# Two gathers of a mixture-of-experts pair, from both sides of an up stage to behind it and to the end of the pair

## The chip, the cores and the metric

The kernel runs on one core of a Trainium2 chip. The metric is the device time of one execution in microseconds (us); less is better. The core has a matrix engine (TensorE, PE in the profile), a vector engine (VectorE, DVE), an activation engine (ScalarE, ACT), a general one (GpSimd, POOL) and a queue that issues the weight loads (SyncE, SP). PEld is TensorE's loading of the stationary operand.

## The reference, cut to what matters

Two decoder layers run on 512 tokens of width 1024. Each has a mixer, a cross-attention to 256 memory tokens and a mixture of experts. The change touches the last alone:

```python
xs = xf[tok]
h = jax.nn.silu(lax.ragged_dot(xs, w_gate, sizes)) * lax.ragged_dot(xs, w_up, sizes)
y = lax.ragged_dot(h, w_down, sizes) * weights.reshape(-1)[order][:, None]
out = jax.ops.segment_sum(y, tok, num_segments=T)
```

There are 32 experts in a layer, and each token goes to two of them. An expert has three float32 matrices of 2 MB (`w_gate`, `w_up` of 1024x512, `w_down` of 512x1024).

## The kernel before, in words

**Pairs and stages.** Experts are taken two at a time: 16 pairs `q` in a layer, 64 token slots for each expert. A pair has six weight stages, two units of 1 MB each (one for each of its experts): GATE part 0 and 1, UP part 0 and 1, DOWN part 0 and 1, below G0, G1, U0, U1, D0, D1. A stage is 16 matmuls with 64 stationary columns; the two experts take the two halves of the array (`hidden_in`, L771; `down`, L786).

**The ring.** All weights come through a ring of six units, so of three stages. SP issues the loads in order (L500), and the two loads of stage s+3 wait for the count `stage_used`, which TensorE raises at the end of stage s. So the end of D1 releases the load of the next pair's U0, the end of G0 that of U1, G1 that of D0, U0 that of D1, U1 that of the next G0, and D0 that of the next G1.

**Gathers.** Two pairs make a batch `b`. Its tokens are brought into slot order by four gathers of 16 matmuls each (one-hot `oh` against the two halves `xnh`, `xnl` of the normed input; `gather`, L741), each into PSUM bank GATHER and copied from there to `xg` by ScalarE (`gathered`, L1242). Each pair `q` of batch b does two of the four gathers of batch b+1. Pairs 14 and 15 have no next batch and do none, so 14 pairs of each layer, 28 in all, have two gathers. A gather waits until the copy before it has left the bank (`xg_ready`).

**The rest of a pair.** After G0 and after U0 come two result mixes each of the pair before (`mix`, L763, 4 matmuls each, which VectorE adds to `x`, L1737). After U1 VectorE makes the hidden values (`hide`, L1721), TensorE transposes them (`hidden_T`, L778), then does the slot weights (L748) and slot transposes (L755) of the next pair while ScalarE copies the hidden values back (`hidden_copy`, L1224), which D0 needs. After D1 ScalarE and VectorE split the results in two halves (L1227, L1733), which the first mix after the next G0 needs.

**Order.** Every engine's order is written out by hand in its own `pair(q)`. TensorE's order before is: G0, mix, mix, G1, U0, mix, mix, first gather, U1, second gather, hidden transposes, slot weights, slots, D0, D1.

Of the kernel before, what the change touches and what calls it, by code (L numbers as in the profile page):

```python
# [54 lines left out]
GATE, UP, TURN, Y, GATHER, MIX, SEL = 0, 1, 2, 3, 5, 6, 6  # L55
# [83 lines left out]
def program(nc, A, out):  # L139
    ctx = ExitStack()  # L140
    with ctx:
# [250 lines left out]
        def after(eng, s, n):  # L392

            if not isinstance(n, int) or n > 0:
                eng.wait_ge(s, n)
# [18 lines left out]
        def took(name):  # L414
            return taken[ROUND[name] % 2]
# [107 lines left out]
        def _(pe):  # L523
# [211 lines left out]
            def gather(b, bank, block):  # L735

                for kk in range(2):
                    k = 2 * block + kk
                    for m in range(TM):
                        for i, a in enumerate((xnh, xnl)):  # L740
                            mm = pe.matmul(ps[:, bank, kk * 256:(kk + 1) * 256], a[:, m, k * P:(k + 1) * P],  # L741
                                           oh[:, b % 2, m, :], start=(m == 0 and i == 0), stop=(m == TM - 1 and i == 1))
                return mm
# [47 lines left out]
            def experts(l):  # L791
# [13 lines left out]
                def do_gather(b, block, bank):  # L805
                    if block == 0:
                        pe.wait_ge(S["oh_ready"], b0 + b + 1)
                    if bank == GATHER:
                        after(pe, S["xg_ready"], 4 * (b0 + b) + block)
                    gather(b, bank, block).then_inc(S["x_gathered"], 1)  # L810
# [39 lines left out]
                def do_down(q, part):  # L850
                    if part == 0:
                        pe.wait_ge(S["hT_ready"], q0 + q + 1)
                        after(pe, S["y_added"], 4 * (q0 + q))
                    down(part, loaded(q, 4 + part)).then_inc(stage_used, 1)

                def pair(q):
                    b = q // 2
                    more = b + 1 < BATCHES
                    do_hidden(q, GATE, 0)
                    if q:  # L860
                        do_mix(q - 1, 0, MIX)
                        do_mix(q - 1, 1, Y)
                    else:
                        do_gather(0, 3, Y + 1)
                        do_slots(0)
                        do_weights(0)
                    do_hidden(q, GATE, 1)
                    do_hidden(q, UP, 0)
                    if q:
                        do_mix(q - 1, 2, MIX)  # L870
                        do_mix(q - 1, 3, Y)
                    if more:
                        do_gather(b + 1, 2 * (q % 2), GATHER)
                    if q == 0 and l + 1 < LAYERS:
                        pe.wait_ge(S["selT_ready"], q0 + 1)
                        pe.wait_ge(S["ws_masked"], 1)
                        pe.wait_ge(S["xg_ready"], 4 * b0 + 4)
                        for g in range(C_GROUPS):
                            mm = pe.transpose(ps[:, MIX + g // 4, (g % 4) * P:(g % 4 + 1) * P], wsn[:, g, :], ident[:, :])
                        mm.then_inc(S["ws_turned"], 1)  # L880
                    do_hidden(q, UP, 1)
                    if more:
                        do_gather(b + 1, 2 * (q % 2) + 1, GATHER)
                    pe.wait_ge(S["h_ready"], q0 + q + 1)
                    after(pe, S["hT_ready"], q0 + q)
                    hidden_T().then_inc(S["hT_done"], 1)
                    if q + 1 < PAIRS:
                        do_weights(q + 1)
                        do_slots(q + 1)
                    do_down(q, 0)  # L890
                    do_down(q, 1)

                pe.wait_ge(S["xn_lo"], l + 1)
                do_gather(0, 0, GATHER)
# [55 lines left out]
            for l in range(LAYERS):  # L950
# [8 lines left out]
                b = begin(("logits", l, 0))  # L959
# [3 lines left out]
                b = begin(("rank", l, 0))  # L963
# [14 lines left out]
        def _(act):  # L978
# [247 lines left out]
            def results_hi():  # L1226
                return act.activation(yh[:, :], ps[:, Y:Y + 2, :].rearrange("p a n -> p (a n)"), ACT.Copy)  # L1227

            def experts(l):
                q0, b0 = PAIRS * l, BATCHES * l  # L1230
                for m in range(TM):
                    act.activation(xnh[:, m, :], xn[:, m, :], ACT.Copy).then_inc(S["xn_hi"], 1)
                b = round_done(act, ("route", l, 0))
                act.activation(lgT[:, :], ps[0:GROUPS + EXPERTS, b, :], ACT.Copy).then_inc(took(("route", l, 0)), 1)
                act.wait_ge(S["g_sub"], l + 1)
                act.activation(gee[:, :, :], ge[:, :, :], ACT.Exp).then_inc(S["g_exp"], 1)
                act.wait_ge(S["e_sub"], l + 1)
                act.activation(ex[:, :, :], ed[:, :, :], ACT.Exp).then_inc(S["e_exp"], 1)

                def gathered(b, block, bank):  # L1240
                    act.wait_ge(S["x_gathered"], 4 * (b0 + b) + block + 1)
                    act.activation(xg[:, b % 2, 2 * block:2 * block + 2, :],  # L1242
                                   ps[:, bank, :].rearrange("p (k n) -> p k n", n=4 * SLOTS), ACT.Copy)\
                       .then_inc(S["xg_ready"], 1)

                def pair(q):
                    b = q // 2
                    more = b + 1 < BATCHES
                    if q == 0:
                        gathered(0, 3, Y + 1)  # L1250
                    act.wait_ge(stage_used, STAGES * (q0 + q) + 2)
                    after(act, S["h_ready"], q0 + q)
                    silu().then_inc(S["silu_done"], 1)
                    if more:
                        gathered(b + 1, 2 * (q % 2), GATHER)
                    if q == 0 and l + 1 < LAYERS:
                        act.wait_ge(S["ws_turned"], 1)
                        act.activation(wsT[:, :, :], ps[:, MIX:MIX + 2, :].rearrange("p a (g n) -> p (a g) n", n=P),
                                       ACT.Copy).then_inc(S["wsT_ready"], 1)
                    act.wait_ge(S["hT_done"], q0 + q + 1)  # L1260
                    after(act, stage_used, STAGES * (q0 + q))
                    hidden_copy().then_inc(S["hT_ready"], 1)
                    if more:
                        gathered(b + 1, 2 * (q % 2) + 1, GATHER)
                    act.wait_ge(stage_used, STAGES * (q0 + q + 1))
                    after(act, S["mixed"], 4 * (q0 + q))
                    results_hi().then_inc(S["yh_ready"], 1)

                gathered(0, 0, GATHER)
                gathered(0, 1, Y)  # L1270
                gathered(0, 2, MIX + 1)
                for q in range(PAIRS - 1):
                    pair(q)
                act.wait_ge(S["tab_ready"], l + 1)
                n = act.value_load(mosti[0:1, 0:1], min_val=0, max_val=T)
                pair(PAIRS - 1)
                with act.If(n > SLOTS):
                    with act.Fori(1, PASSES) as c:
                        with act.If(n > c * SLOTS):
                            with act.Fori(0, PAIRS) as e:  # L1280
                                at_ = lambda k: c * (OVER * PAIRS) + e * OVER + (1 - OVER * PAIRS + k)
                                act.wait_ge(over_step[l], at_(4))
                                act.activation(xg[:, 0, :, 0:P],
                                               ps[:, MIX:MIX + 2, :].rearrange("p a (k n) -> p (a k) n", n=P), ACT.Copy)\
                                   .then_inc(over_step[l], 1)
                                act.wait_ge(over_step[l], at_(10))
                                silu().then_inc(over_step[l], 1)
                                act.wait_ge(over_step[l], at_(14))
                                hidden_copy().then_inc(over_step[l], 1)
                                act.wait_ge(over_step[l], at_(16))  # L1290
                                results_hi().then_inc(over_step[l], 1)
                            act.wait_ge(over_step[l], c * (OVER * PAIRS) + 1)
                            settle(act)
                        act.nop()
                act.nop()
# [712 lines left out]
```

## Time and profile before

| | us |
|---|---|
| median of 3 runs | 2151.8 (2149.51 to 2153.68) |
| the profiled execution's own time | 2144.74 |
| its span, first to last instruction | 2143.0 |
| TensorE busy | 1951.5 (91%) |
| TensorE waits for weights that an UP stage needs | 21.4, in 27 waits |
| TensorE waits for weights that a GATE stage needs | 4.3, in 5 waits |

The span is what the trace covers; the time of an execution has some 2 us around it. A busy share says how long an engine worked, not that it set the end. The mean granted TensorE clock is 0.957 of full speed over the span. The weights of the experts are 384 loads of 1 MB, of 491 MB that the DMA engines moved in all.

### The profile page before, as it was taken

Reading aid. Unit: us, or ns where it says so; the run is one execution under the profiler, and the core shown is the slowest. Engines: PE = TensorE matmul, PEld = TensorE weight load, DVE = VectorE, ACT = ScalarE, POOL = GpSimd, SP = SyncE. Lnnn points to the kernel's source line nnn. Section 1 sums busy time; section 2 is a strip of 40 time slices with the busy share of each in tenths; the row PEclk is TensorE's granted clock in tenths of the full one; section 3 lists DMA queues with packets and bytes.
Section 4 is the critical chain, followed back from the end, with each engine's and each line's share of the span. In section 5 each row is a group of like instructions: output and inputs, shape, how many; then the busy total and the mean of one; then the engine's idle time right before and its main releaser. Section 6 shows DMA issues by size and latency. Waiting matters only on the chain.

```text
span 2143.0 us, 22950 instructions
## 1 busy us (share of the span) xinstructions
PE 1951.5 (91%) x9528; PEld 1255.3 (59%) x9528; DVE 784.6 (37%) x1201; ACT 525.4 (25%) x941; POOL 114.8 (5%) x131
## 2 busy tenths in 40 slices
PE   6987899986999999999799979989878999999997
PEld 5865577665545444444388869977565444444443
DVE  3356455435123222222433253364352222222222
ACT  3246333423111011110234332334331011101100
POOL 2100010002000000000100031000010000000000
PEclk9998899997999999999899989999988999999999
DMA  6210232211699999999732312332014999999997
GB/s 219 98 59 1 79 109 98 79 42 59 263 398 412 401 404 397 403 394 407 308 104 91 134 35 79 104 123 99 23 59 187 407 405 390 414 391 398 399 405 292
DMA packets 100139, 491.15 MB, mean 229 GB/s; under 512 B 7720, under 2 KB 15960, under 8 KB 50752
## 3 DMA queue, kind: packets, MB, share of 16 engines
q1 hardware_dynamic: 96928, 478.18, 56.8%
q0 software_dynamic: 2512, 9.33, 1.3%
q8 instruction: 80, 1.31, 0.3%
q10 hardware_dynamic: 592, 2.11, 0.3%
q14 instruction: 27, 0.22, 0.0%
HBM read 487.47 MB, written 2.10 MB: 228 GB/s over the span
## 4 chain that ended last, share of the span: by engine, by line
PE 73%; DMA 12%; DVE 8%; ACT 3%; issue 2%; POOL 1%; SPq 0%; ACTq 0%; DVEq 0%; POOLq 0%
PE ps L551 24%; PE ps L771 12%; DMA ring<-in_moe_w_up 12%; PE ps L786 11%; PE ps L741 6%; PE ps L548 5%; PE ps L763 3%; PE ps L726 1%; PE ps L719 1%; PE ps L564 1%; PE ps L581 1%; PE ps L657 1%; PE ps L603 1%; DVE wl L443 1%; PE ps L755 1%
## 5 line engine op out<-in xcount | busy, mean ns | idle before, releaser
L771 PE MATMUL ps<-ring,xg 128*64 128x512 f32 x2048 | 465.8, 596 | 26.1 <-DMA ring<-in_moe_w_up 21.4
L443 DVE TENSOR_TENSOR wl<-ring,wh 128x512 fp32r<-128x512 f32 x280 | 192.0, 695 | 409.7 <-ACT wh L434 408.8
L771 PEld LDWEIGHTS ps<-ring,xg 128*64 128x64 f32 x2048 | 146.0, 136 | 299.5 <-issue 295.4
L434 ACT ACTIVATE wh<-ring 128x512 fp32r<-128x512 f32 x280 | 174.8, 630 | 447.6 <-PE ps L551 361.9
L1737 DVE TENSOR_TENSOR x<-ps,x 128x1024 f32<-128x1024 f32 x128 | 150.6, 1220 | 305.0 <-PE ps L763 305.0
L786 PE MATMUL ps<-ring,hT 128*64 128x512 f32 x1024 | 230.3, 602 | 1.4 <-ACT hT L1224 1.4
L551 PE MATMUL ps<-wh,ah 128*128 128x512 f32 x544 | 216.7, 398 | 13.0 <-DVE al L1444 6.2
L551 PE MATMUL ps<-wl,ah 128*128 128x512 f32 x544 | 215.5, 396 | 0.0
L551 PE MATMUL ps<-wh,al 128*128 128x512 f32 x544 | 214.7, 395 | 0.0
L786 PEld LDWEIGHTS ps<-ring,hT 128*64 128x64 f32 x1024 | 71.5, 138 | 137.5 <-issue 130.6
L741 PE MATMUL ps<-oh,xnh 128*128 128x256 f32 x512 | 131.6, 294 | 5.2 <-DVE oh L1755 5.2
L741 PE MATMUL ps<-oh,xnl 128*128 128x256 f32 x512 | 127.7, 287 | 0.0
L551 PEld LDWEIGHTS ps<-wh,ah 128*128 128x128 f32 x544 | 104.4, 192 | 37.9 <-DVE al L1444 8.2
L1733 DVE TENSOR_TENSOR yl<-ps,yh 128x1024 fp32r<-128x1024 f32 x32 | 39.2, 1225 | 230.9 <-ACT yh L1227 230.9
L741 PEld LDWEIGHTS ps<-oh,xnh 128*128 128x128 f32 x512 | 99.1, 194 | 32.5 <-issue 31.4
L551 PEld LDWEIGHTS ps<-wh,al 128*128 128x128 f32 x544 | 104.5, 192 | 22.3
L551 PEld LDWEIGHTS ps<-wl,ah 128*128 128x128 f32 x544 | 104.5, 192 | 21.8
L763 PE MATMUL ps<-yh,selT 128*128 128x512 f32 x256 | 106.9, 417 | 4.8 <-DVE yl L1733 4.8
L763 PE MATMUL ps<-yl,selT 128*128 128x512 f32 x256 | 100.6, 393 | 0.0
L741 PEld LDWEIGHTS ps<-oh,xnl 128*128 128x128 f32 x512 | 99.2, 194 | 1.2
L1242 ACT ACTIVATE xg<-ps 128x512 f32<-128x512 f32 x64 | 38.0, 594 | 249.3 <-PE ps L741 249.3
L1721 DVE SCALAR_TENSOR_TENSOR hh<-ps,wcol,sg 128x512 f32<-128x512 f32 x32 | 36.7, 1146 | 139.9 <-PE ps L771 139.9
(248 smaller groups left out, 2464.2 us busy)
## 6 DMA issues: line engine op xcount, KB each, us to landing
ring<-in_moe_w_gate SPq DMA_DIRECT2D x128, 1024.0 KB, 7.1
ring<-in_moe_w_up SPq DMA_DIRECT2D x128, 1024.0 KB, 8.8
ring<-in_moe_w_down SPq DMA_DIRECT2D x128, 1024.0 KB, 9.6
ring<-in_x_wkv SPq DMA_DIRECT2D x16, 1024.0 KB, 5.1
ring<-in_c_w_in SPq DMA_DIRECT2D x16, 1024.0 KB, 5.3
ring<-in_ab_w_in SPq DMA_DIRECT2D x10, 1024.0 KB, 13.2
ring<-in_x_wq SPq DMA_DIRECT2D x8, 1024.0 KB, 5.0
ring<-in_x_wo SPq DMA_DIRECT2D x8, 1024.0 KB, 5.0
```

What stands on the lines that cost most here:

```text
L434: act.activation(wh[:, t % STAGE, :], ring[:, unit % RING, 512 * s:512 * (s + 1)], ACT.Copy).then_inc(wh_ready, 1)
L443: dve.tensor_tensor(wl[:, t % STAGE, :], ring[:, unit % RING, 512 * s:512 * (s + 1)], wh[:, t % STAGE, :].bitcast(F32), ALU.subtract).then ...
L548: mm = pe.matmul(ps[:, b + m, 0:T], w[:, t % STAGE, m * P:(m + 1) * P], a[:, k, :], **flags)
L551: mm = pe.matmul(ps[:, b + m, 0:cols], a[:, k, m * P:(m + 1) * P], w[:, t % STAGE, kk * cols:(kk + 1) * cols], **flags)
L741: mm = pe.matmul(ps[:, bank, kk * 256:(kk + 1) * 256], a[:, m, k * P:(k + 1) * P], oh[:, b % 2, m, :], start=(m == 0 and i == 0), stop=(m ...
L763: mm = pe.matmul(ps[:, bank + half, :], selT[:, q % 2, m * P:(m + 1) * P], a[:, 512 * half:512 * (half + 1)], start=(i == 0), stop=(i == 1))
L771: mm = pe.matmul(ps[p * SLOTS:(p + 1) * SLOTS, bank, :], xg[:, b % 2, k, r * P + p * SLOTS:r * P + (p + 1) * SLOTS], w(p)[:, k % 4, :], st ...
L786: mm = pe.matmul(ps[p * SLOTS:(p + 1) * SLOTS, Y + half, :], hT[:, k, p * SLOTS:(p + 1) * SLOTS], w(p)[:, k % 2, 512 * half:512 * (half + 1)],
L1242: act.activation(xg[:, b % 2, 2 * block:2 * block + 2, :], ps[:, bank, :].rearrange("p (k n) -> p k n", n=4 * SLOTS), ACT.Copy)\
L1721: return dve.scalar_tensor_tensor(out=hh[:, :].rearrange("p (k c) -> p k c", k=KF), in0=by_row(ps[:, UP, :]), scalar=wcol[:, 0:1], in1=by_ ...
L1733: return dve.tensor_tensor(yl[:, :], ps[:, Y:Y + 2, :].rearrange("p a n -> p (a n)"), yh[:, :].bitcast(F32), ALU.subtract)
L1737: return dve.tensor_tensor(x[:, m, :], ps[:, bank:bank + 2, :].rearrange("p a n -> p (a n)"), x[:, m, :], ALU.add)
```

## The change

In TensorE's order the first gather of a pair goes from in front of U1 to behind it, where the second one stood, and the second goes behind D1, in front of the next pair's G0. ScalarE's copies follow: the first one stands where it was (behind `silu`, now also behind the copy of `wsT` in pair 0), the second goes from behind `hidden_copy` to behind `results_hi`. Nothing is added or taken away.

```diff
                     if q:
                         do_mix(q - 1, 2, MIX)
                         do_mix(q - 1, 3, Y)
-                    if more:
-                        do_gather(b + 1, 2 * (q % 2), GATHER)
                     if q == 0 and l + 1 < LAYERS:
...
                     do_hidden(q, UP, 1)
                     if more:
-                        do_gather(b + 1, 2 * (q % 2) + 1, GATHER)
+                        do_gather(b + 1, 2 * (q % 2), GATHER)
                     pe.wait_ge(S["h_ready"], q0 + q + 1)
...
                     do_down(q, 0)
                     do_down(q, 1)
+                    if more:
+                        do_gather(b + 1, 2 * (q % 2) + 1, GATHER)
...
                     silu().then_inc(S["silu_done"], 1)
-                    if more:
-                        gathered(b + 1, 2 * (q % 2), GATHER)
                     if q == 0 and l + 1 < LAYERS:
                         act.wait_ge(S["ws_turned"], 1)
...
+                    if more:
+                        gathered(b + 1, 2 * (q % 2), GATHER)
                     act.wait_ge(S["hT_done"], q0 + q + 1)
                     after(act, stage_used, STAGES * (q0 + q))
                     hidden_copy().then_inc(S["hT_ready"], 1)
-                    if more:
-                        gathered(b + 1, 2 * (q % 2) + 1, GATHER)
                     act.wait_ge(stage_used, STAGES * (q0 + q + 1))
                     after(act, S["mixed"], 4 * (q0 + q))
                     results_hi().then_inc(S["yh_ready"], 1)
+                    if more:
+                        gathered(b + 1, 2 * (q % 2) + 1, GATHER)
```

## Rows read from the trace of the kernel before

**Rows 1.** The profile page: an engine's busy time, and the span in 40 slices.

```profile
PE 1951.5 (91%) x9528; PEld 1255.3 (59%) x9528; DVE 784.6 (37%) x1201; ACT 525.4 (25%) x941; POOL 114.8 (5%) x131
...
DMA  6210232211699999999732312332014999999997
```

**Rows 2.** Windows: pairs 2 to 13 of each layer (stretch; length, busy; clock, DMA share, GB/s).

```profile
599.30:976.00 376.70, 368.13 (x1873) 178.93 (x1873) 103.95 (x114) 39.65 (x60) 0.00 (x0) 1.00 0.98 401
1680.30:2058.10 377.80, 368.14 (x1873) 179.11 (x1873) 103.89 (x114) 39.66 (x60) 0.00 (x0) 1.00 0.98 401
```

**Rows 3.** The chain that ended last, one pair (start us, us, what).

```profile
602.68 7.02 PE ps L786 x32
609.70 3.43 PE ps L771 x16
613.13 2.04 PE ps L763 x8
615.17 3.58 PE ps L771 x16
...
618.82 3.65 PE ps L771 x16
...
624.53 1.92 PE ps L741 x16
626.45 3.58 PE ps L771 x16
630.03 2.10 PE ps L741 x16
...
633.42 1.86 PE ps L786 x7
```

**Rows 4.** The chain's DMA steps behind two of the D1 stages: shortest, longest.

```profile
734.60 8.72 DMA ring<-in_moe_w_up
...
828.33 10.41 DMA ring<-in_moe_w_up
```

**Rows 5.** TensorE's DMA waits, 599.3 to 976.0 (us in total, times, longest).

```profile
PE ps L771 <- DMA ring<-in_moe_w_up: 7.8, 10, 1.3
PE ps L771 <- DMA ring<-in_moe_w_gate: 0.5, 1, 0.5
```

**Rows 6.** The same, 1680.3 to 2058.1.

```profile
PE ps L771 <- DMA ring<-in_moe_w_up: 8.4, 11, 1.3
PE ps L771 <- DMA ring<-in_moe_w_gate: 1.1, 2, 0.8
```

**Rows 7.** The same, the first two pairs of layer 0.

```profile
PE ps L771 <- DMA ring<-in_moe_w_up: 1.3, 1, 1.3
```

**Rows 8.** Windows: behind a D0 stage, inside the pairs, and at a layer's end.

```profile
730.00:734.00 4.00, 4.00 (x20) 1.29 (x18) 0.00 (x0) 0.00 (x0) 0.00 (x0) 1.00 0.70 240
...
740.00:790.00 50.00, 49.32 (x260) 25.13 (x258) 13.82 (x18) 5.58 (x9) 0.00 (x0) 1.00 1.00 414
990.00:1040.00 50.00, 44.10 (x196) 17.92 (x197) 13.88 (x14) 3.41 (x5) 0.00 (x0) 0.98 1.01 422
```

**Rows 9.** Timeline of TensorE from the second gather's end to D0.

```profile
725.59 0.28 PE L741 MATMUL ps<-oh,xnl 128*128 128x256 f32 x1
725.71 0.60 PE L778 MATMUL ps<-ident,hh 128*128 128x128 f32 x4
...
727.10 0.65 PE L786 MATMUL ps<-ring,hT 128*64 128x512 f32 x2
```

**Rows 10.** Timeline of ScalarE in the same stretch.

```profile
726.35 0.60 ACT L1224 ACTIVATE hT<-ps 128x512 f32<-128x512 f32 x1 [5.52 <-PE ps L778]
726.84 0.59 ACT L1242 ACTIVATE xg<-ps 128x512 f32<-128x512 f32 x1
```

**Rows 11.** Timeline of VectorE behind the same U1.

```profile
723.83 1.15 DVE L1721 SCALAR_TENSOR_TENSOR hh<-ps,wcol,sg 128x512 f32<-128x512 f32 x1 [4.08 <-PE ps L771]
```

## The prediction

> **What bounds the kernel now.** I read the page first. TensorE is busy 91% of the span, and the DMA line stands at 9 in two blocks of slices, which are the expert parts of the two layers [rows 1]. So there two resources are near their limits at once, and a share of the span can't say which of them sets the pace. I therefore cut out pairs 2 to 13 of each layer, all with two gathers, from the end of one U1 to the end of another [rows 2]: 376.7 and 377.8 us, so 754.5 us for 24 pairs, 31.44 us a pair. TensorE is busy for 736.3 of them, 30.68 a pair, at full granted clock. The DMA engines show a share of 0.98 and 401 GB/s. A pair needs 12 MB, that is 12.58 million bytes; if the 0.02 of idle share were filled, the rate would be 401 / 0.98 = 409 GB/s and a pair's weights would take 30.75 us. So both could do a pair in about 30.7 us, and it takes 31.4: each now and then waits for the other.
>
> The chain shows where. In a pair in which the weights come just in time it is TensorE's own work from end to end, 602.68 to 633.42, 30.74 us [rows 3]. In most pairs it leaves TensorE: from the end of D1 through the DMA load of the next U0, which lands 8.72 to 10.41 us after its issue [rows 4], to that U0. Without a wait U0 would begin 3.43 + 2.04 + 3.58 = 9.05 us after D1 (G0, two mixes, G1) [rows 3]. The second of its two loads is issued 0.4 us behind the end of D1, so it is there 9.1 to 10.8 us after D1, and nearly always late. The waits of TensorE confirm it: 7.8 us in ten waits for UP weights in twelve pairs, 8.4 us in eleven in layer 1, and 1.6 us for GATE weights in both [rows 5, 6].
>
> Why does this load land late? It is released by the end of D1, and the loads of G1, released by the end of D0, are still in front of it in the queue. The queue itself had run dry a moment before: 730 to 734 us, around the release by a D0, shows a share of 0.70 and 240 GB/s, against 414 and 422 GB/s in longer stretches [rows 8]. The releases come unevenly. From U0's end to U1's end two mixes, a gather and U1 pass, 2.05 + 1.92 + 3.58 = 7.6 us, and from U1's to D0's about 7.0, both with loads of 5 us to be paid for; then D0, D1, G0 come 3.4 us apart, faster than the queue can serve.
>
> **The change part by part.** Nothing is removed: 32 gather matmuls a pair stay, 16 of them behind D1.
>
> *The wait for U0.* Between D1 and U0 there is now a gather as well. It takes 2.10 us behind a weight stage, and G0 behind a gather takes 3.58, as G1 does behind a mix, in place of 3.43 [rows 3]. U0 begins 2.10 + 3.58 + 2.04 + 3.58 = 11.3 us after D1. Its second load was there after 10.8 us at the latest. All of this wait goes. A stage that begins with a wait also takes 3.65 us and one that follows on directly 3.43 [rows 3], so each removed wait gives 0.22 us more.
>
> *What is late next.* The loads follow each other at about 2.5 us per MB (1.049 million bytes at 422 GB/s [rows 8]), 5.0 a stage. If U0's weights land at 9.8 after D1 (the middle of the above), U1's, released by G0 at 5.7, land at 14.8, and U1 begins at 11.3 + 3.43 + 2.05 = 16.8, 2.0 us later. D0's land at 19.8 and are needed at 23.8 (U1, gather, then 1.3 us up to D0). D1's land at 24.8, needed at 27.4. The next G0's at 29.8, needed at 32.9. The next G1's, released at 27.4, are there by 35 and needed at 38.5. So nothing is late by the mean; the smallest margin is U1's 2.0 us. What was the long gap before U1 is 5.6 us now, and the gather fills the short one between D1 and G0. I see no stage that takes the wait over at full price.
>
> *What it costs on TensorE.* Each pair has one change of matmul shape more in each direction: G0 3.58 for 3.43, and the first gather behind U1 at 2.10 in place of 1.92 behind a mix: 0.15 + 0.18 = 0.33 us [rows 3]. A sentence of the Trainium skill speaks against the change here: TensorEngine Tiling (Array Packing), Key Properties, says that a change of tiling mode drains TensorE. If each of the two added changes cost a whole restart as after a wait, 0.22 us by the rows, the sum would be 0.44 a pair and the gain 3 us less; I go by the rows' 0.33.
>
> *The copies.* The first gather's copy now stands in front of `hidden_copy` on ScalarE. The gather ends at 725.87, the copy could begin at 725.90, and ScalarE takes its next instruction 0.49 us after it (726.35 to 726.84), so `hidden_copy` begins at 726.39 instead of 726.35 [rows 9, 10]. D0 begins 0.15 us after it ends, so D0 is 0.04 us later. From below this is 0, from above, if the copy had to end first, 0.15. I take 0.04. `hide` on VectorE takes 1.15 us and is covered by the gather behind U1 as before, 2.1 us [rows 11]; without this cover it would cost 1.2 a pair, but a gather of the same size stays there. The second copy waits behind `results_hi`, about 1.0 us after D1, and its gather ends at 2.1; it is needed only in G1 of an even pair, 7.7 us after D1, and by the next gather, behind U1. `results_hi` itself loses the copy in front of it, which was long done. The mix behind G0 gets 2.25 us more time for its split. All these at nothing. The reordering around `wsT` happens once, in pair 0 of layer 0, under U1: nothing.
>
> *The sum.* A pair without any wait would be D0 and D1 7.02, gather 2.10, G0 3.58, mixes 2.04, G1 3.58, U0 3.43, mixes 2.05, U1 3.58, gather 2.10, hidden transposes to slots 1.29 (632.13 to 633.42), and 0.04: 30.81 us. Against 31.44 that is 0.63 us a pair, 15.1 for 24 pairs. Pair 1 of each layer has one wait of 1.3 [rows 7] (taken for layer 1 as well): 1.3 + 0.22 - 0.37 = 1.15 each; pair 0 has none and pays 0.37. That is 1.6 for four pairs, 16.7 in all. But 30.81 stands only 0.06 above what the DMA share gives for the weights, 30.75. With limits this close, single late loads still make TensorE wait. The load behind D1 varied by 1.7 us [rows 4], against margins of 2.0 and more, so most are taken up; I charge 3.2 us over 28 pairs, about a sixth of what the waits are now, which is a choice and not a reading. The ends for this term are 0 and, if the queue sets the pace at 31.1 a pair, 8. The gain is 13.5 us.
>
> The profiled execution took 2144.74 us, its span 2143.0. The sum says 2129.5 for the span and 2131.2 for its time. The median of the runs is 7.1 us above the profiled time; I carry the same gain over to it: 2151.8 - 13.5 = 2138.3.
>
> **The rivals.** A change under 0.2%, 4.3 us, is what a measurement of this kernel can't tell from none.
>
> *The queue is the bound and the gain is small.* If 401 to 405 GB/s is all that this flow gives, a pair stays at 31.1 to 31.4 us and the gain is 0 to 8 us, say 3: 2149. For it: the share of 0.98 leaves little idle time. Against it: 414 GB/s over 50 us within the pairs and 422 at the layer's end, where TensorE waits more [rows 8].
>
> *The shape changes and ScalarE's order cost more.* All that can be saved is 2 x 1.3 + 17.8 us of waits and 26 restarts of 0.22 [rows 5 to 7], 26.1 us, 0.93 a pair. Two matmuls on an empty array take 0.65 us [rows 9], their steps within a stage 3.43 / 16 = 0.21 each. If each added change cost the 0.4 us by which the one is above the other, and the copy its 0.15, the costs were 0.95: 2152. Against it: the changes that are there already stand in rows 3 at 0.15 and 0.18.
>
> *Slower.* The place is the two new borders, D1 to gather and gather to G0, and it decides from costs of 0.93 us a pair. If TensorE stood still at each for the whole 0.65 us [rows 9], the costs would be 1.30 and the kernel 28 x 0.37 = 10 us slower: 2162. No border in the trace has this price.
>
> *More gain.* Margins of 2 us take up every late load, and the end of each layer, pairs 14 and 15, profits from the queue's lead: 18 to 20 us, 2133.
>
> **How the numbers follow.** Forecast (gain 8 to 17 us) 0.68; queue-bound small gain 0.16 (half of it under 4.3); shape changes eat it 0.05; slower 0.04; more gain 0.07. Faster is 0.68 + 0.08 + 0.07 = 0.83, same 0.08 + 0.05 = 0.13, slower 0.04. The range takes in the queue-bound half that shows and the larger gain: 2131 to 2147.
>
> **What would show it.** In the profile after: TensorE's waits for UP weights in pairs 2 to 13 fall from 16.2 us to under 4; the two stretches take 370 us each; G0 takes 3.58 and both gathers 2.1; DMA share is at 1.00 and 408 GB/s or more; D0 begins no more than 0.1 us later behind the gather. It would be wrong if the waits came back in front of U1 or G1, if a gather behind D1 took clearly more than 2.1 us, or if the GB/s stayed at 401.

## The result and the profile after

The changed kernel takes 2127.8 us (median of 4 runs, 2126.2 to 2135.6) against 2151.5 us, ratio 0.990 with a 95% interval of 0.9877 to 0.9923. That is 23.7 us less. The forecast was 2138.3 us, a gain of 13.5, with a range down to 2131: the direction was right, and the gain was under-sized by 10 us. Two more sets of runs of the same kernel, told below, gave 0.9901 and 0.9903, with medians 20.7 and 17.7 us below those of the kernel before beside them. Over all executions on record the median is 2150.4 us before (73, from 2137.1 to 2160.4) and 2129.3 after (15, from 2124.1 to 2135.6). So the gain is about 21 us, and the 23.7 of the first medians is the largest of the three.

The two profiled executions lie closer together: their spans are 2143.0 and 2133.8 us, 9.2 apart. This gap between what the profiles say and what the medians say is what the runs had to settle. The profiled execution of before (2144.7 us) was one of its faster ones, and that of the changed kernel (2135.6 us) the slowest of its 15.

Windows of the changed kernel first: pairs 2 to 13 of each layer, then the whole expert part of each layer, from the first G0 to the end of the last U1. The columns are those of [rows 2]: stretch; length, busy time of each engine; clock, DMA share, GB/s.

```profile
600.00:971.40 371.40, 370.23 (x1875) 175.44 (x1873) 103.97 (x114) 39.69 (x60) 0.00 (x0) 1.00 1.00 408
1675.40:2046.40 371.00, 369.90 (x1873) 175.19 (x1873) 103.98 (x114) 39.69 (x60) 0.00 (x0) 1.00 1.00 408
551.10:1032.20 481.10, 477.19 (x2405) 223.70 (x2404) 129.15 (x144) 52.62 (x78) 0.00 (x0) 1.00 0.99 403
1626.40:2107.50 481.10, 475.95 (x2397) 222.81 (x2396) 129.12 (x144) 51.59 (x77) 0.00 (x0) 1.00 0.99 403
```

The same view of the kernel before, whole expert parts:

```profile
547.10:1035.80 488.70, 474.79 (x2405) 227.60 (x2404) 129.09 (x144) 52.58 (x78) 0.00 (x0) 1.00 0.97 397
1629.20:2117.90 488.70, 474.09 (x2397) 227.04 (x2396) 129.10 (x144) 51.55 (x77) 0.00 (x0) 1.00 0.97 397
```

Pairs 2 to 13 take 371.4 and 371.0 us in place of 376.7 and 377.8 [rows 2], and TensorE is busy for all but a microsecond of them. The DMA share went from 0.98 to 1.00. The whole parts give 2 x 7.6 = 15.2 us back, so between these two executions 6.0 us were lost outside them: the first G0 begins at 551.1 instead of 547.1, and the stretches between and behind the expert parts are 2 us longer. It doesn't follow the change: in the two later profiles of the changed kernel, span less expert parts is 1168.2 and 1161.6 us, here 1171.6, and in the three of before 1165.5 to 1166.9.

One pair on the chain that ended last, changed kernel (start us, us, what; the cut leaves out slot weights and slots):

```profile
724.11 2.09 PE ps L741 x16
726.20 0.44 PE ps L778 x4
...
727.49 7.02 PE ps L786 x32
734.51 2.08 PE ps L741 x16
736.59 3.58 PE ps L771 x16
740.18 2.04 PE ps L763 x8
742.22 3.58 PE ps L771 x16
745.80 0.11 issue
745.91 3.65 PE ps L771 x16
749.57 2.04 PE ps L763 x8
751.61 3.58 PE ps L771 x16
```

The chain stays on TensorE through the whole pair, where before it left for the load of U0 [rows 4]. Each term is where it was forecast: both gathers 2.1, G0 3.58. In this pair 0.11 us is left in front of U0, and U0 takes the 3.65 us of a stage behind a wait. TensorE's waits for expert weights over the whole kernel, at the end of the costliest row of the groups by line:

```profile
L771 PE MATMUL ps<-ring,xg 128*64 128x512 f32 x2048 | 463.6, 597 | 6.6 <-DMA ring<-in_moe_w_up 4.6 <-DMA ring<-in_moe_w_gate 1.6
```

That is 6.2 us, where there were 25.7. The 4.6 us for UP weights are eight waits, all in front of U0; the longest, in the timeline of TensorE:

```profile
1666.09 3.65 PE L771 MATMUL ps<-ring,xg 128*64 128x512 f32 x16 [0.98 <-DMA ring<-in_moe_w_up]
```

ScalarE behind the first gather, timeline of the changed kernel:

```profile
726.24 0.60 ACT L1242 ACTIVATE xg<-ps 128x512 f32<-128x512 f32 x1 [10.72 <-PE ps L741]
726.73 0.59 ACT L1224 ACTIVATE hT<-ps 128x512 f32<-128x512 f32 x1
```

The copy stands in front of `hidden_copy`, 0.49 us ahead of it, as worked out from [rows 10]. TensorE ends the gather at 726.19 and begins D0 at 727.42, 1.23 us later, the same as before [rows 9]. The 0.04 us that I charged for it doesn't show in this pair.

### The profile page after: what moved, and what is told of

Same layout as the page of the kernel before. It is cut to its first block, busy times and chain, and to the rows that moved or that the text cites. A ratio compares the mean times of both kernels' runs of the same rounds, so it can differ in the third digit from the quotient of the medians.

```text
span 2133.8 us, 22950 instructions
## 1 busy us (share of the span) xinstructions
PE 1962.4 (92%) x9528; PEld 1249.7 (59%) x9528; DVE 784.9 (37%) x1201; ACT 525.7 (25%) x941; POOL 115.2 (5%) x131
## 4 chain that ended last, share of the span: by engine, by line
PE 81%; DVE 8%; DMA 4%; ACT 4%; issue 2%; POOL 1%; SPq 0%; DVEq 0%; ACTq 0%; POOLq 0%
PE ps L551 24%; PE ps L771 19%; PE ps L786 11%; PE ps L741 6%; PE ps L548 5%; PE ps L763 5%; DMA ring<-in_moe_w_up 4%; PE ps L726 1%; PE ps L719 1%; PE ps L581 1%; PE ps L564 1%; PE ps L657 1%; DVE wl L443 1%; PE ps L603 1%; PE ps L652 1%
## 5 line engine op out<-in xcount | busy, mean ns | idle before, releaser
L771 PEld LDWEIGHTS ps<-ring,xg 128*64 128x64 f32 x2048 | 140.9, 136 | 272.7 <-issue 268.6
L1227 ACT ACTIVATE yh<-ps 128x1024 fp32r<-128x1024 f32 x32 | 32.9, 1027 | 235.0 <-PE ps L786 235.0
```

Source lines behind the costliest of these rows:

```text
L771: mm = pe.matmul(ps[p * SLOTS:(p + 1) * SLOTS, bank, :], xg[:, b % 2, k, r * P + p * SLOTS:r * P + (p + 1) * SLOTS], w(p)[:, k % 4, :], st ...
```

## The experiments

All ratios are to the kernel before, run on the same chip.

**Both kernels again.** No edit.

> The changed kernel once more, with no edit. Theory A (the change is worth what the removed waits for U0 are worth, and the profiled executions show it): the expert parts, from the first gate stage to the last up stage, take 481 us a layer as in the first profile of this kernel (488.7 before), so 15 us together; the time is 15 us under that of before, ratio 0.993, and the 24 us of the first medians was partly spread between executions. Theory B (in most executions of the kernel before the waits are longer than in its one profile, because late loads strike it harder): the ratio stays at 0.990 or below, and profiles of before taken again show more than 488.7 us a layer.

> The kernel before once more, with no edit, as the measure of spread: ratio 1.000 within 0.002. Theory A: its expert parts take 488.7 us a layer within 1 us, as in the first profile (2143.0 us span). Theory B: they take 490 us or more a layer and the span is 2147 to 2152, the first profile having been a lucky one.

> The kernel before, profiled a third time. If the difference between its executions is the waits of the expert parts (first profile: span 2143.0, waits for expert weights 25.7 us; second: 2153.0 and 34.0), then this span lies at about 2143 + (waits - 25.7) x 1.2, within 3 us. If the spans and the waits don't go together, the spread comes from the dense parts.

> The changed kernel a third time, beside the other on the same chip. Theory A: ratio 0.990 within 0.002, expert parts of 480.5 to 481.5 us a layer, waits for expert weights of 5 to 7 us, as in both profiles of it so far, while those of before differ by 10.

| kernel | profiled span | waits for expert weights | two expert parts | median time, ratio (interval) |
|---|---|---|---|---|
| before | 2143.0 | 25.7 | 488.7 + 488.7 | 2151.5 |
| before_again | 2153.0 | 34.0 | 493.7 + 492.4 | 2151.8 beside 2149.7, 1.0011 (0.9993 to 1.0029) |
| before_third | 2153.1 | 35.9 | 493.5 + 494.1 | 2154.9, one run |
| after | 2133.8 | 6.2 | 481.1 + 481.1 | 2127.8 beside 2151.5, 0.990 (0.9877 to 0.9923) |
| after_again | 2129.4 | 6.1 | 480.8 + 480.4 | 2129.0 beside 2149.7, 0.9901 (0.9872 to 0.9931) |
| after_third | 2124.7 | 6.4 | 483.6 + 479.5 | 2130.4 beside 2148.1, 0.9903 (0.987 to 0.9937) |

The list of TensorE's waits of before_again, and of before_third (us in total, times, longest):

```profile
PE ps L771 <- DMA ring<-in_moe_w_up: 27.2, 30, 1.3
...
PE ps L771 <- DMA ring<-in_moe_w_gate: 6.8, 9, 2.2
```

```profile
PE ps L771 <- DMA ring<-in_moe_w_up: 27.3, 28, 1.3
...
PE ps L771 <- DMA ring<-in_moe_w_gate: 8.6, 12, 1.4
```

Theory B holds, though the span of before_again is 1 us beyond what it said. The profile that I had read was of an execution with fewer waits than the two others: of the 10 us by which each of their spans is longer, 8.7 and 10.2 lie in the expert parts. For before_third the sum from its waits was 2143.0 + 10.2 x 1.2 = 2155.2, measured 2153.1. The changed kernel hardly varies there (962.2, 961.2 and 963.1 us for both parts), with the same 6 us of waits each time. So the gain in the expert parts is 15 us against the first profile of before and 24 to 25 us against the other two. A usual execution lies between: the first profiled one took 2144.7 us, the other two 2154.9 each, and the median of all is 2150.4. The three differences of medians, 23.7, 20.7 and 17.7 us, lie between 15 and 24 as well. after_third missed its expectation in one layer part each way (483.6 and 479.5 where 480.5 to 481.5 was said).

**TensorE's own work, without the weights.** Half of each unit is loaded, in either order. The kernels leave out the other half of every expert's weights, so their output isn't the reference's and they serve for the time alone. Before, the last of these lines loaded `slot(u, cols)` whole and the middle one wasn't there.

```python
src, cols = expert_unit(l, q, j)
half = 2 if cols == 512 else 1
sp.dma_start(slot(u, cols)[:, 0:half], src[:, 0:half]).then_inc(ring_full[u % RING], 16)
```

> The order of the kernel before, with half of each expert unit loaded (512 KB of 1 MB; the other half of the slot keeps what an earlier unit left, so the output of the experts is not the reference's). The weight queue then has twice the time it needs, and TensorE never waits for weights. Theory A (TensorE's own work is 30.44 us a pair in this order): expert parts of 14 x 30.44 plus the tail, pairs 2 to 13 in 365.3 us, no waits for expert weights, and a spread between executions far under the 17 us of the full kernel. If the pair stays near 31 us, the time lost before is not for weights at all.

> The same half loads in the order of the changed kernel. Theory A (the order costs TensorE 0.31 to 0.37 us a pair for one change of matmul shape more in each direction, and pays only because of the weights): pairs 2 to 13 in 369.0 us, 3.7 to 4.4 us more than with the order of before, and the whole kernel 9 to 10 us slower than light_before. Rival (the order itself is better for TensorE, and the weights had little part in the gain): faster than light_before.

Windows of light_before, pairs 2 to 13 and the whole parts:

```profile
601.70:967.00 365.30, 365.30 (x1875) 177.12 (x1873) 103.96 (x114) 39.71 (x60) 0.00 (x0) 1.00 0.63 207
...
551.10:1023.40 472.30, 471.07 (x2405) 225.32 (x2404) 129.12 (x144) 52.65 (x78) 0.00 (x0) 1.00 0.63 207
1612.60:2083.90 471.30, 470.08 (x2397) 224.45 (x2396) 129.11 (x144) 51.63 (x77) 0.00 (x0) 1.00 0.63 208
```

And of light_after:

```profile
600.10:969.00 368.90, 368.90 (x1873) 174.57 (x1873) 103.97 (x114) 39.72 (x60) 0.00 (x0) 1.00 0.63 205
...
551.10:1027.60 476.50, 475.28 (x2406) 222.53 (x2404) 129.15 (x144) 52.67 (x78) 0.00 (x0) 1.00 0.63 205
1616.00:2091.30 475.30, 474.08 (x2397) 221.77 (x2396) 129.14 (x144) 51.64 (x77) 0.00 (x0) 1.00 0.63 206
```

With the weights never late, a pair takes 365.3 / 12 = 30.44 us in the old order and 368.9 / 12 = 30.74 in the new. Times: 2109.8 us, ratio 0.9801 (0.9777 to 0.9824), and 2117.6, 0.9839 (0.9815 to 0.9863). Neither has a wait for expert weights. The new order is the worse one for TensorE, by 0.30 us a pair and 8.2 us in both parts (I had said 9 to 10 us for the kernel; the medians differ by 7.7). The spread is smaller too. As the range grows with the number of runs, here are standard deviations: 2.0 and 2.6 us with half loads (6 runs each), 3.3 in the changed kernel (15), 5.0 in the kernel before (73). From this the account of the gain, for the two expert parts:

| | TensorE alone | with all weights | the weights cost |
|---|---|---|---|
| before (first profile) | 943.6 | 977.4 | 34 |
| before (again, third) | 943.6 | 986.1, 987.6 | 43 |
| after (three profiles) | 951.8 | 961.2 to 963.1 | 10 |

So 24 to 33 us of lateness are removed, by which profile of before one takes, and 8 are paid for it. For a gain of 21 us it is 29 us, an estimate.

**The change in two halves.** both_behind_u1 takes the first gather out of the gap before U1 and puts nothing behind D1. In this diff and the next ones ScalarE's copies are left out; they move with their gathers.

```diff
-                    if more:
-                        do_gather(b + 1, 2 * (q % 2), GATHER)
...
                     do_hidden(q, UP, 1)
+                    if more:
+                        do_gather(b + 1, 2 * (q % 2), GATHER)
                     if more:
                         do_gather(b + 1, 2 * (q % 2) + 1, GATHER)
```

> From the kernel before: the first gather stands behind U1 too, directly in front of the second. Half of the change alone: the gap from U0 to U1 is 5.6 us as in the changed kernel, but nothing stands between D1 and G0. The second gather waits for the first one's copy, at 0.7 us a pair. Theory A: U0 still begins 9.05 us after D1 and waits, 0.6 us or more a pair as before, so the gain is absent and the 0.7 us a pair is added: 28 x 0.7 = 20 us slower, ratio 1.007 to 1.012. Rival (the long gap before U1 was what starved the queue): the waits for UP weights fall under 5 us and the ratio is 1.000 within 0.003.

2164.2 us, ratio 1.0078 (1.0049 to 1.0108). TensorE's waits:

```profile
PE ps L741 <- ACT xg L1242: 19.2, 28, 0.7
...
PE ps L771 <- DMA ring<-in_moe_w_up: 16.6, 27, 1.3
```

The second gather waits 0.7 us for the first one's copy 28 times, as expected, and the waits for UP weights are still there, 27 of them: shortening the gap before U1 alone doesn't cure them. In the timeline of TensorE 19 of them, 12.8 us, stand in front of U0, where before all 27 stood (21.4 us), and 8, 3.9 us, in front of U1. So a part of the wait has moved to U1, and what is left at U0 is under the 0.6 us a pair that I expected there.

second_behind_d1 leaves the first gather in front of U1 and moves the second behind D1:

```diff
                     do_hidden(q, UP, 1)
-                    if more:
-                        do_gather(b + 1, 2 * (q % 2) + 1, GATHER)
...
                     do_down(q, 1)
+                    if more:
+                        do_gather(b + 1, 2 * (q % 2) + 1, GATHER)
```

> The other half of the change alone: the first gather stays in front of U1, the second goes behind D1, and nothing stands between U1 and the hidden transposes. By the distances from a release to the stage that needs its load (G0 11.6, G1 11.2, U0 11.3, U1 13.0 us or more) no stage waits for weights, but hide on VectorE (1.15 us) is uncovered: 7.02 + 2.10 + 3.58 + 2.04 + 3.58 + 3.43 + 2.05 + 1.92 + 3.58 + 1.21 + 1.29 = 31.8 us a pair, all of it TensorE's and VectorE's. Against 31.4 to 31.8 before: 0 to 11 us slower, ratio 1.000 to 1.005, with waits for weights under 3 us in pairs 2 to 13. If the cover isn't needed, 30.8 us a pair and a ratio of 0.990.

2166.2 us, ratio 1.0066 (1.0044 to 1.0089), a little beyond what was expected. Its chain behind a U1:

```profile
731.03 1.12 DVE hh L1721
732.15 0.04 issue
732.19 0.66 PE ps L778 x4
```

The waits for weights fall to 4.1 + 1.4 us, but `hide` is bare in every pair, 38.8 us in 32 waits, and the transposes behind it take 0.66 us in place of 0.44, the restart that my sum of 31.8 us lacked: the windows give 32.1 and 32.2. One could object that the weights are in time only because the pair has become longer. The other half settles this, for its pairs are as long. Windows of pairs 2 to 13, first both_behind_u1, then second_behind_d1:

```profile
601.90:988.70 386.80, 371.18 (x1873) 178.36 (x1873) 103.83 (x114) 39.65 (x60) 0.00 (x0) 1.00 0.96 392
```

```profile
602.50:988.10 385.60, 370.45 (x1874) 176.61 (x1872) 103.41 (x114) 41.04 (x60) 0.00 (x0) 1.00 0.98 392
```

At 386.8 and 385.6 us the queue has about the same time for the same weights, and TensorE's waits for them over the whole kernel are 20.6 us in the one (16.6, 3.4 and 0.6 for UP, GATE and DOWN) and 5.5 us in the other. So the gather behind D1 is what cures U0, and the first gather has to move behind U1 because the second one leaves `hide` without a cover. Neither half is faster than before; together they are 1% faster.

**Is any even spacing as good?** first_before_g1 lengthens the way from D1 to U0 with the first gather in front of G1, at no extra change of shape:

```diff
                         do_mix(q - 1, 1, Y)
...
+                    if more:
+                        do_gather(b + 1, 2 * (q % 2), GATHER)
                     do_hidden(q, GATE, 1)
                     do_hidden(q, UP, 0)
                     if q:
                         do_mix(q - 1, 2, MIX)
                         do_mix(q - 1, 3, Y)
-                    if more:
-                        do_gather(b + 1, 2 * (q % 2), GATHER)
```

> From the kernel before: the first gather of a pair stands behind the two mixes that follow G0 and in front of G1, the second stays behind U1. U0 then begins 3.43 + 2.04 + 1.92 + 3.58 = 11.0 us after D1, without a border between matmul shapes more than before. Theory A (the wait for U0 is a matter of the distance D1 to U0): the waits for UP weights fall from 21 us to under 5, TensorE needs 30.4 us a pair where the changed kernel needs 30.75, and the weight queue now sets the pace at 30.7 to 30.9: 2127 to 2131, ratio 0.989 to 0.992, as the changed kernel or 1 to 3 us better. Rival (only the place behind D1 helps, because there the gather gives the queue time between the releases of D1 and G0): the waits stay at 15 us or more and the ratio at 0.997 or above.

2143.4 us, ratio 0.9967 (0.9949 to 0.9984), so less than half of the gain. Its waits:

```profile
PE ps L771 <- DMA ring<-in_moe_w_gate: 14.3, 18, 2.4
...
PE ps L771 <- DMA ring<-in_moe_w_up: 7.0, 10, 1.2
```

Theory A missed: it had said 2131 at most. The rival's ratio came out, 0.997, but not by its reason, for the waits for UP weights fell from 21 us to 7. The wait for U0 is gone in most pairs and has moved to G0: all 18 waits for GATE weights stand directly behind D1, as here in the timeline of TensorE.

```profile
699.76 7.09 PE L786 MATMUL ps<-ring,hT 128*64 128x512 f32 x32
707.47 3.65 PE L771 MATMUL ps<-ring,xg 128*64 128x512 f32 x16 [0.63 <-DMA ring<-in_moe_w_gate]
```

The way from U1, which releases G0's load, to G0 is 2.10 + 1.29 + 7.02 = 10.4 us here; in the changed kernel the gather behind D1 makes it 12.5.

mixes_behind_u1 also moves the second two mixes behind U1, and `hide` in front of VectorE's last two adds:

```diff
-                    if q:
-                        do_mix(q - 1, 2, MIX)
-                        do_mix(q - 1, 3, Y)
...
                     do_hidden(q, UP, 1)
+                    if q:
+                        do_mix(q - 1, 2, MIX)
+                        do_mix(q - 1, 3, Y)
```

> A third order, from the kernel before: the first gather behind the two mixes in front of G1 (as in first_before_g1), the other two mixes and then the second gather behind U1; VectorE does hide in front of its last two adds. G0 to D1 then stand 12.5, 10.8, 11.0, 11.0, 12.1 and 12.4 us behind the ends that release their loads, none of them under 10.8, and there is one change of matmul shape less in each direction than before: TensorE needs 30.1 us a pair, the changed kernel 30.75. Theory A (what counts is that no distance is short, and with that the weight queue is the floor): the waits don't collect at G0 as in first_before_g1, and the time is that of the changed kernel or up to 4 us under it, 2124 to 2131, ratio 0.987 to 0.991, not the 18 us under it that 28 x 0.65 would give. Rival (a gather between D1 and G0 is needed): 2140 or more, ratio 0.996.

2143.7 us, ratio 0.9977 (0.9954 to 0.9999): theory A missed by some 13 us, and the rival's 2140 or more came true. Its chain:

```profile
700.16 7.02 PE ps L786 x32
707.18 3.46 PE ps L771 x16
...
711.03 11.34 DMA ring<-in_moe_w_up
722.36 0.14 issue
722.50 3.65 PE ps L771 x16
```

All distances were 10.8 us or more, and U1 waits in nearly every pair (33.0 us for UP weights). D0, D1 and G0 follow each other directly, 3.4 us apart, and each releases 2 MB that the queue needs 5 us for. D0's end, the middle of the first row, is at 703.7; from there to U1's start TensorE has 3.4 + 3.5 + 11.0 = 17.9 us of work, while U1's weights, the third stage in line, land at 722.37, 18.7 us later. In the changed kernel that way is 3.43 + 2.08 + 3.58 + 2.04 + 3.58 + 3.43 + 2.04 = 20.2 us. So I read it thus: it is not each distance that counts but the work up to each of the next three stages, counted from the start of a run of quick releases. This is read from these two chains, and no run was made to test it. The order with the least TensorE work of all, 30.1 us a pair by its sum, is 13 us slower than the changed kernel beside it (2130.4). None of the other orders beats it.

## Why the prediction was right or wrong

**What bounds it: right.** The wait for U0, caused by 9.05 us of work between D1 and U0, was the loss, and behind it the queue stood close. The forecast of 30.75 us for a pair's weights is what the kernel now runs into: 12.58 MB at 408 GB/s and a share of 1.00 is 30.8 us, and TensorE's own pair 30.74.

**TensorE's costs: right.** 0.33 us for the two borders between shapes (0.30 in the half-load kernels), 0.04 for the copy (measured 0), 30.81 us a pair (30.74). Covers held: `hide` behind the first gather, the second copy before G1.

**What is late next: right that no stage takes the wait over, wrong on the smallest margin.** I called U1's 2.0 us the smallest, but my own figures give U0 less: 11.3 against a landing at 9.8, so 1.5 us, and 0.5 us against the latest, 10.8. "All of this wait goes" was too much. The eight waits for UP weights that are left, 4.6 us in all, are all at U0, and none is at U1. In pairs 2 to 13 they are 2.0 us, where I had said under 4.

**The charge for single late loads: right where it was meant, partly by luck.** For the profiled execution the sum was 13.5 us and the expert parts gave 15.2. In pairs 2 to 13 the gain is 12.1 us, where 15.1 less my charge for them, 2.7, makes 12.4. Two errors cancel in it: TensorE needs 30.74 us a pair and not 30.81, and the late loads cost 4.6 us and not 2.7 (371.4 and 371.0 against 368.9 with half loads). What the sum lacks for this execution lies mostly at the layer's ends: pairs 14 and 15, which have no gathers and were in no term, waited 5.3 us for weights before and 3.3 after.

**The step that failed** is the one in which the profiled execution was taken for all: "The median of the runs is 7.1 us above the profiled time; I carry the same gain over to it." Those 7.1 us were not a constant on top. They were for the most part more of the very waits that the change removes: 34.0 and 35.9 us in the later profiles of before, 25.7 in the one I read, and of the 10 us by which those spans are longer 8.7 and 10.2 lie in the expert parts. So the term "wait for U0" was too small: by 9 to 10 us for the two later profiles, and by 5 us for a usual execution, an estimate from its time, 2150.4 against 2144.7. With the 1.7 us that the sum lacked already this makes the gain 20 to 21 us, and 21 was measured. The first medians, at 23.7 us, then lie beyond that by their own spread. My range of 2131 to 2147 was built on the spread of causes and not on the spread between executions of before.

**The rivals.** The queue as a bound with little gain: wrong, though the queue is the bound now. Shape changes that eat the gain, and slower: wrong, 0.30 us a pair against the 0.93 from which they would have decided. "More gain", at 0.07, named 18 to 20 us and came nearest. One of its reasons, the layer's ends, gave 1 to 2 us of it; the late loads were not all taken up, and the spread of before was not in it.

What stays open: why the queue delivers a little less in some executions of before (397 against 401 GB/s in pairs 2 to 13). The smaller spread of the half-load kernels speaks for the weight loads as the source of most of it; what delays single loads wasn't tried.

## What to carry to other kernels

When a ring of buffers is refilled on release, look at when the releases come and not only at the total work. Quick stages in a row ask for several loads at once, and the last of them can be late even if the queue has time over the whole cycle; work that waits for nothing, such as a gather for the next batch, belongs into that run, and it may be worth an extra change of matmul shape. Where the profiled time lies under the median of the runs, ask which wait could be what is missing: if it is the wait that the change removes, the gain in the median is larger than in the profile. One profile of each kernel can't tell this; two more of each did.

## What the runs showed of the hardware that was not expected

With TensorE alone as the limit, twelve pairs took 365.3 us in both layers and 368.9 us in both layers of the other order: its pace repeats to within 0.1 us in 365, at a granted clock of 1.00. Most of the spread between executions went with the weight loads: a standard deviation of 5.0 us with all of them in the order before, 2.0 with half. The queue held 422 GB/s over 50 us at a layer's end [rows 8] but 408 over 371 us with its share at 1.00. And the restart of 0.22 us behind a wait showed again where nothing was streamed from the ring: four transposes of 0.44 us took 0.66 behind the wait for `hide`.
